# Expert stage with 160 slots per expert and a quarter-row tail, and a last stage written out tile by tile

## What is computed

```python
gp = softmax(hf @ w_group + b_group);  g_w, g_idx = top_k(gp, 1)
el = (hf @ w_router + b_router).reshape(T, 4, 8) taken at g_idx
e_val, e_idx = top_k(el, 2);  gate = softmax(e_val) * g_w      # 2 of 32 experts a token
y = (silu(xb @ w_gate[e]) * (xb @ w_up[e])) @ w_down[e]        # 1024 -> 512 -> 1024
h = h + sum of gate * y over the token's two experts
out = rms_norm(h, final_norm_w)
```

## Time and profile before

| | us |
|---|---|
| median of 3 runs | 1985.79 (1985.59 to 1987.25) |
| the profiled execution | 1985.4 |
| its span | 1983.6 |
| PE busy | 1793.7 (90%) |
| DVE / ACT / POOL busy | 619.7 / 501.0 / 231.4 |
| mixer, routing and first gather, experts, last stage | 0 to 1006, to 1060, to 1874, to 1983.6 |

### The profile page before, as it was taken

The page is one execution under the profiler, slowest core; times in us unless marked ns, Lnnn a source line. Parts: engine busy times, 40 slices in busy tenths (PEclk is TensorE's granted clock), DMA queues, the critical chain, the costliest instruction groups (busy, mean ns, idle before and its releaser), DMA issues.

```text
span 1983.6 us, 29788 instructions
## 1 busy us (share of the span) xinstructions
PE 1793.7 (90%) x10758; PEld 1285.1 (65%) x10759; DVE 619.7 (31%) x1155; ACT 501.0 (25%) x1173; POOL 231.4 (12%) x319
## 2 busy tenths in 40 slices
PE   7999999999999999999837999999999999999700
PEld 4656666656666656666426778887887888888500
DVE  1333323333224333324362222222221222222265
ACT  0433434233424333333300111111111111111121
POOL 0000101100101100101011000000000000000175
PEclk9999999999999999999858999999999999999955
DMA  9522112222012222022175788888887988888576
GB/s 324 135 85 86 36 50 84 85 85 85 23 62 85 85 85 75 21 73 85 64 271 168 261 302 294 281 303 306 300 304 263 318 303 299 301 296 291 185 255 222
DMA packets 194491, 358.65 MB, mean 181 GB/s; under 512 B 12179, under 2 KB 81444, under 8 KB 194452
## 3 DMA queue, kind: packets, MB, share of 16 engines
q1 hardware_dynamic: 183812, 320.93, 47.8%
q0 software_dynamic: 10640, 37.17, 6.2%
HBM read 280.73 MB, written 77.33 MB: 181 GB/s over the span
## 4 chain that ended last, share of the span: by engine, by line
PE 39%; issue 5%; DVE 2%; POOL 2%; DMA 1%; ACT 1%; POOLq 0%; ACTq 0%; SPq 0%; DVEq 0%
PE bank L1075 12%; PE bank L1100 11%; PE bank L1064 11%; PE bank L1049 3%; PE bank L1089 1%; POOL wts L1211 1%; DMA wts<-y_dram,dc 1%; POOL fs L1220 0%; DVE column L945 0%; ACT sg L1109 0%; DVE place L945 0%; DVE y L1135 0%; PE bank L350 0%; POOL dc L1207 0%; DMA y_dram<-y 0%
## 5 line engine op out<-in xcount | busy, mean ns | idle before, releaser
L282 PE MATMUL bank<-w_in_sb,uT 128*128 128x512 f32 (+1 forms) x1024 | 379.8, 524 | 4.8 <-DMA w_in_sb<-w_in_in 4.8
L282 PEld LDWEIGHTS bank<-w_in_sb,uT 128*128 128x128 f32 x1024 | 176.6, 192 | 173.3 <-issue 167.2
L1064 PEld LDWEIGHTS bank<-xT,wts 128*128 128x128 f32 x2048 | 250.1, 192 | 33.0 <-issue 26.6
L1064 PE MATMUL bank<-xT,wts 128*128 128x128 f32 (+2 forms) x2048 | 256.1, 285 | 11.9 <-issue 8.6
L1075 PE MATMUL bank<-xT,wts 128*128 128x128 f32 (+2 forms) x2048 | 247.9, 282 | 0.0
L1075 PEld LDWEIGHTS bank<-xT,wts 128*128 128x128 f32 x2048 | 245.0, 191 | 0.0
L1100 PE MATMUL bank<-wts,hT 128*128 128x512 f32 x512 | 233.5, 599 | 0.0
L430 PE MATMUL bank<-w_out_sb,mixT 128*128 128x512 f32 x512 | 224.0, 596 | 0.8 <-ACT mixT L507 0.8
L1128 DVE TENSOR_TENSOR hT<-bank,sg 128x256 f32<-128x256 f32 x128 | 54.3, 424 | 445.3 <-PE bank L1075 445.3
L430 PEld LDWEIGHTS bank<-w_out_sb,mixT 128*128 128x128 f32 x512 | 96.7, 191 | 116.7 <-issue 116.7
L1100 PEld LDWEIGHTS bank<-wts,hT 128*128 128x128 f32 x512 | 92.1, 190 | 99.7 <-issue 97.6
(11 more groups left out here) (206 smaller groups left out, 1722.1 us busy)
## 6 DMA issues: line engine op xcount, KB each, us to landing
wts<-w_gate_in SPq DMA_DIRECT2D x32, 2048.0 KB, 9.6
wts<-w_up_in SPq DMA_DIRECT2D x32, 2048.0 KB, 8.7
wts<-w_down_in SPq DMA_DIRECT2D x32, 2048.0 KB, 10.5
y_dram<-nought SPq DMA_DIRECT2D x64, 512.0 KB, 6.0
y_dram<-y SPq DMA_DIRECT2D x32, 512.0 KB, 10.4
x_sb<-x_in SPq DMA_DIRECT2D x17, 512.0 KB, 4.0
w_in_sb<-w_in_in SPq DMA_DIRECT2D x4, 2048.0 KB, 12.4
h_sb<-x_in SPq DMA_DIRECT2D x16, 512.0 KB, 6.0
```

Source lines behind the costliest of these rows:

```text
L282: m = pe.matmul(bk[name][:, col:col + hi - lo], uT[:, k, :], w_in[:, k, lo:hi], start=k == 0, stop=k == KD - 1)
L1064: m = pe.matmul(G[m_ % 2][:, 0:w], wg[:, k, m_ * P:(m_ + 1) * P], xT[:, k, 0:w], start=k == 0, stop=k == KD - 1)
```

## The change

1. An expert has MAIN = 160 main slots. Rows past 160 go to an overflow block (NOV 25 instead of 16; NCOL 114 instead of 96). `WIDTHS` has 128, 144, 160 only. The part of `y` between slot 160 and 256 and both halves of the overflow blocks are cleared: 6 DMAs of 512 KB a tile instead of 4.
2. The tail (slots 128 to 159) is gathered as 128 quarter rows of 1 KB, on 128 partitions: partition 32 q + r gets quarter q of row r. The index for it is 4 token + q, made in routing by one more matmul with a new constant `rep` and three more DVE instructions.
3. PE then transposes 8 pieces of the main part and 2 of the tail, in three steps of 4, 4 and 2. Step 0 stands between up and down, steps 1 and 2 between the halves of down. DVE evacuates with two instructions of 512 and two of 128 columns.
4. POOL and SP don't read the class: POOL always issues a gather of 128 rows and one of 128 quarter rows, SP always stores 512 KB and four times 32 KB. `y`'s second half is written by ACT alone (256 columns).
5. The last stage has no loop. POOL uses `dest` itself as index; the mean goes to ACT (`scale` in the square, epsilon by an Identity); DVE uses `gates` itself. POOL issues gathers three tiles ahead.

The core of the diff (names of helpers and waits left out where they only follow):

```diff
+MAIN = 160
+NOV = 25
-WIDTHS = (P, P + TAIL // 2, P + TAIL, CAP)
+WIDTHS = (P, P + TAIL // 2, MAIN)
...
-            for b in (2 * (n * i + m) + 1, 2 * NE + n * i + m):
+            for b in (2 * (n * i + m) + 1, 2 * NE + 2 * (n * i + m), 2 * NE + 2 * (n * i + m) + 1):
...
+        pe.wait_ge(sem("idx_tail_ready"), 1)
+        pe.matmul(bank[3][:, 0:NE], rep[:, 0:P], idx_f[:, :], start=True, stop=True).then_inc(sem("idx_spread"), 1)
...
-        dve.tensor_copy(idx, bank[2][:, 0:NCOL]).then_inc(sem("idx_ready"), 1)
+        dve.tensor_copy(idx[:, 0:NCOL:2], bank[2][:, 0:NCOL:2]).then_inc(sem("idx_ready"), 1)
+        dve.tensor_copy(idx_f[:, :], bank[2][:, 1:2 * NE:2]).then_inc(sem("idx_tail_ready"), 1)
+        dve.tensor_copy(idx[:, 2 * NE + 1:NCOL:2], bank[2][:, 2 * NE + 1:NCOL:2])
+        v_.wait_ge(sem("idx_spread"), 1)
+        dve.tensor_scalar(idx[:, 1:2 * NE:2], bank[3][:, 0:NE], 4.0, rep[:, P:P + 1], ALU.mult, ALU.add)\
+            .then_inc(sem("idx_ready"), 1)
...
+    def store(sp, e):
+        stored = sem("m_y_stored")
+        sp.dma_start(rows_of(e * CAP, P), y[:, 0, :]).then_inc(stored, 16)
+        for j in range(4):
+            sp.dma_start(rows_of(e * CAP + P, TAIL)[:, j * CAP:(j + 1) * CAP], yt[j * TAIL:(j + 1) * TAIL, :]).then_inc(stored, 16)
...
+    def gather(po):
+        po.indirect_dma_start(out=xg[:, 0, :], in_=scratch["v2"], out_offset=None,
+                              in_offset=bass.IndirectOffsetOnAxis(ap=idxc[:, 0:1], axis=0)).then_inc(sem("m_xg_loaded"), 16)
+        po.indirect_dma_start(out=xt, in_=scratch["v2"].rearrange("t (q c) -> (t q) c", q=4), out_offset=None,
+                              in_offset=bass.IndirectOffsetOnAxis(ap=idxc[:, 1:2], axis=0)).then_inc(sem("m_xt_loaded"), 16)
...
+    def pe_x(pe, n, steps):
+        for j in steps:
+            if j == 0:
+                wait(pe, sem("m_xg_loaded"), 16 * (n + 1))
+                after(pe, "m_", "xT_ready", 3 * n)
+            if j == 2:
+                wait(pe, sem("m_xt_loaded"), 16 * (n + 1))
+                after(pe, "m_", "xT_ready", 3 * n + 1)
+            for c in range(4 if j < 2 else 2):
+                src = xg[:, 0, (4 * j + c) * P:(4 * j + c + 1) * P] if j < 2 else xt[:, c * P:(c + 1) * P]
+                m = pe.transpose(XB[j % 2][:, c * P:(c + 1) * P], src, ident)
+            m.then_inc(sem("m_x_done"), 1)
...
-        next_x((0, 1))
+        next_x((0,))
...
-                next_x((2, 3))
+                next_x((1, 2))
...
+    def pool_tiles(po):
+        def fetch(t):
+            b = t % NYG
+            wait(po, sem("sum_s_ready"), t - NYG + 1)
+            for n in range(2):
+                po.indirect_dma_start(out=yg[:, b, n, :], in_=scratch["y"], out_offset=None,
+                                      in_offset=bass.IndirectOffsetOnAxis(ap=dest[:, n * NT + t:n * NT + t + 1], axis=0))\
+                    .then_inc(sem(f"yg_loaded{b}"), 16)
+        for t in range(NYG - 1):
+            fetch(t)
+        for t in range(NT):
+            if t + NYG - 1 < NT:
+                fetch(t + NYG - 1)
+            po.wait_ge(sem("fmean_ready"), t + 1)
+            nc.gpsimd.tensor_tensor(fs[:, t, 1:2], fs[:, t, 0:1], fk[:, 1:2], ALU.pow).then_inc(sem("froot_ready"), 1)
+    def act_tiles(act):
+        act.wait_ge(sem("fk_ready"), 2)
+        for t in range(NT):
+            wait(act, sem("sum_s_ready"), t + 1)
+            act.activation(fjunk[:, t % 2, :], hc[:, t, :], ACT.Square, scale=D ** -0.5, accum_out=fs[:, t, 0:1])\
+                .then_inc(sem("fss_ready"), 1)
+            act.wait_ge(sem("fss_ready"), t + 1)
+            act.activation(fs[:, t, 0:1], fs[:, t, 0:1], ACT.Identity, bias=fk[:, 0:1]).then_inc(sem("fmean_ready"), 1)
+    def dve_tiles(v_):
+        def add(t):
+            b, ht = t % NYG, hc[:, t, :]
+            v_.wait_ge(sem(f"yg_loaded{b}"), 32 * (t // NYG + 1))
+            nc.vector.scalar_tensor_tensor(ht, yg[:, b, 0, :], gates[:, t, 0:1], ht, ALU.mult, ALU.add).then_inc(sem("sum_steps"), 1)
+            v_.wait_ge(sem("sum_steps"), t + 1)
+            nc.vector.scalar_tensor_tensor(ht, yg[:, b, 1, :], gates[:, t, 1:2], ht, ALU.mult, ALU.add).then_inc(sem("sum_s_ready"), 1)
+        add(0)
+        for t in range(NT):
+            if t + 1 < NT:
+                add(t + 1)
+            v_.wait_ge(sem("froot_ready"), t + 1)
+            wait(v_, sem(f"out_stored{t % 2}"), 16 * (t // 2))
+            nc.vector.scalar_tensor_tensor(oc[:, t % 2, :], hc[:, t, :], fs[:, t, 1:2], fw[:, :], ALU.mult, ALU.mult)\
+                .then_inc(sem("sum_o_ready"), 1)
```

More of the change, by code:

```diff
@@ L1005, in load @@
         sp.dma_start(dst, src.rearrange("e (k p) n -> p (e k) n", p=P)).then_inc(sem(f"{pre}{name}_loaded"), 16)
[L1007 to L1033, removed]
+    def rows_of(row, n):
+        return scratch["y"][row:row + n, :] if isinstance(row, int) else scratch["y"][bass.ds(row, n), :]
@@ new lines, in gather, with gather_over @@
+    def gather(po):
[3 more added lines that the diff above has]
+                              in_offset=bass.IndirectOffsetOnAxis(ap=idxc[:, 1:2], axis=0)).then_inc(sem("m_xt_loaded"), 16)
+    def gather_over(po):
+        for part in range(2):
+            po.indirect_dma_start(out=xg[:, part, :], in_=scratch["v2"], out_offset=None,
+                                  in_offset=bass.IndirectOffsetOnAxis(ap=idxc[:, part:part + 1], axis=0))\
+                .then_inc(sem("o_xg_loaded"), 16)
@@ L1097, in pe_chunk @@
         for half in range(2):
-            after(pe, pre, ("yA_taken", "yD_taken")[half], 2 * n)
+            after(pe, pre, ("yA_taken", "yD_taken")[half], n if half and pre == "m_" else 2 * n)
             for k in range(KF):
@@ L1112, in act_chunk, with dve_x, dve_x_over @@
             after(act, pre, "d_done", 3 * n + 2 - part)
-            act.activation(y[:, part, 0:512], (YB, G)[part][0][:, :], ACT.Copy).then_inc(sem(pre + "yA_taken"), 1)
-    def dve_x(v_, pre, n, steps):
+            if part and pre == "m_":
+                act.activation(yt, G[0][:, 0:CAP], ACT.Copy).then_inc(sem("m_yA_taken"), 1)
+            else:
+                act.activation(y[:, part, 0:512], (YB, G)[part][0][:, :], ACT.Copy).then_inc(sem(pre + "yA_taken"), 1)
+    def dve_x(v_, n, steps):
+        for j in steps:
+            after(v_, "m_", "x_done", 3 * n + j + 1)
+            after(v_, "m_", "u_done", 4 * n)
+            if j < 2:
+                nc.vector.tensor_tensor(xT[:, 4 * j:4 * j + 4, 0:P], XB[j][:, :].rearrange("p (a b) -> p a b", a=4),
+                                        norm2[:, 4 * j:4 * j + 4].unsqueeze(2).to_broadcast([P, 4, P]), ALU.mult)\
+                    .then_inc(sem("m_xT_ready"), 1)
+            else:
+                for c in range(2):
+                    m = nc.vector.tensor_tensor(xT[:, c::2, P:MAIN], XB[0][:, c * P:(c + 1) * P].rearrange("p (q r) -> p q r", q=4),
+                                                norm2[:, c::2].unsqueeze(2).to_broadcast([P, 4, TAIL]), ALU.mult)
+                m.then_inc(sem("m_xT_ready"), 1)
+    def dve_x_over(v_, n, steps):
+        pre = "o_"
         for j in steps:
@@ L1131, in dve_y @@
     def dve_y(v_, pre, n, part):
-        if part:
+        if part or pre == "m_":
             wait(v_, sem(f"{pre}y_stored"), 80 * (n + 1))
@@ L1287, in program @@
         with ExitStack() as mem:
-            (credit, load, store, clear_xg, gather, copy_index, pe_x, pe_chunk, act_chunk, dve_x, dve_h, dve_y) = \
-                experts(nc, sem, bank, A, K, scratch, weights, mem)
+            (credit, load, store, store_over, gather, gather_over, copy_index, pe_x, pe_x_over, pe_chunk, act_chunk,
+             dve_x, dve_x_over, dve_h, dve_y) = experts(nc, sem, bank, A, K, scratch, weights, mem)
         block = ctx.enter_context(nc.Block())
@@ L1310, in _ @@
             mix_sp_loads(sp)
-            for q in range(2):
-                sp.sem_inc(sem(f"out_stored{q}"), 16)
             for pre in ("m_", "o_"):
```

171 lines of the change are left out of this document (63 added, 108 removed).

## The result

| | before | changed |
|---|---|---|
| time, median of 4 runs | 1986.5 us (1985.6 to 1988.4) | 1942.7 us (1941.1 to 1948.3) |
| ratio, with its 95% interval | | 0.978 [0.976, 0.980] |
| profiled execution: its time, its span | 1985.4, 1983.6 | 1948.3, 1946.3 |
| routing begins (logits), us from the start | 1005.8 | 1008.8 |
| routing and first rows, until the first gate matmul | 53.99 | 54.24 |

What follows compares the result with a forecast made beforehand. PE was taken to bound the experts, with DMA close second, and POOL the last stage. Experts -13.3, routing +0.6 and last stage -14.0 took 1985.4 to 1958.7, so 1959 us; range 1947 to 1975.

Steps and rivals of the forecast that it cites:

- the gain between the halves: Experts, PE: two transposes fewer between the halves of down, with nothing else awaited, save 0.22 us an expert.
- the new wait for `hT`: Ahead of down, PE waits about 0.25 us for DVE; gain 0.17 us (class 128), 0.23 (class 144), not 0.44.
- right to charge 0: Experts, DMA: 15 small packets an engine at 0.09 us, 1.35 us per class 128 expert, just fit; cost 0.
- Rival B: Experts: DMA becomes the limit; packets at 0.33 us give +55, near 2020; mild form 1966. Chances 0.08 mild, 0.04 past the turn.
- its ends: Routing and first rows: net +0.6 us, with ends -2 and +4.
- 333 GB/s when full, and a tile's 1.57 MB take 4.7 us: Last stage: 266 GB/s at share 0.80 was scaled to a full DMA rate, giving a floor per tile.
- the slowest of these is the DMA: Last stage: DMA, not POOL or DVE, sets the pace; 4.85 us a tile instead of 5.91 saves 13.8 us.
- POOL's 4.4 us: Last stage: two gathers and the power, stretched by DVE's scaling and additions, end near 4.4 us a tile.
- DVE's 3 x 1.32 = 4.0: Last stage: DVE's three instructions a tile need 4.0 us.
- POOL sets this: Last stage before the change: POOL, in work or its own issue gaps, sets the 5.91 us between output tiles.
- Rival A: Last stage: POOL and DVE exclude each other, 6.3 us a tile, +5 us instead of -13.8, total about 1978; chance 0.11.
- Rival C: Both hidden costs are smaller: experts -21 us, last stage at 4.4 us a tile (-20), total 1945; chance 0.07.

Runs made afterwards that it cites:

- oc4: The changed kernel with eight transposes ahead of down and two between its halves, plus four output buffers instead of two: 1929.7 us, ratio 0.973.
- dest_copy: The changed kernel with the copy of the two index columns, and the wait for it, on POOL again: 1950.1 us, ratio 0.983.
- mean_pool: The changed kernel with mean and epsilon computed on POOL again: 1951.5 us, ratio 0.984.
- experts_only: The changed kernel with the old last stage (loop, copies, mean on POOL, gathers two tiles ahead): 1970.9 us, ratio 0.992.
- last_only: The kernel before with only the new last stage; experts, classes, clears and routing as before: 1958.5 us, ratio 0.986.
- short_add_oc4: The changed kernel with four output buffers and DVE's second addition cut to 8 of 1024 columns: 1932.8 us, ratio 0.974.

## Why the prediction was right in one half and wrong in the other

**Experts: 13.6 us for 13.3, the mechanism right, so close in part by luck.** The count of ten transposes, the gain between the halves (0.22, measured 4.41 - 4.19 = 0.22) and the new wait for `hT` came as worked out. The semaphore takes 0.13 us, not 0.06 (no row stood behind the 0.06), so the gain ahead of down in class 128 is 0.11 instead of 0.17; class 144 fell from 26.5 to 26.06 us, the 0.45 forecast. Class 128 fell by 0.33 instead of 0.39, class 160 by about 0.5. That makes some 12.4 us. What brings it to 13.6 had no term: the first gate at the low clock, 2.5 us lost, and some 3.7 us gained in the periods of experts 0 to 6 and 16. There PE waits ahead of a gate for something that the profile doesn't name, four times and 8.6 us before, three times and 6.6 us after.

**DMA of the experts: right to charge 0.** The share was forecast at 22.8 / 22.96 = 0.99; it is 0.95 to 0.96. Even the 0.09 us for a small packet was too much. Rival B needed 0.2 us and a wait of PE for weights; the profile names none. (One of the three waits without a name ends at 1091.40, and the `w_gate` load that this gate needs was issued at 1073.54 and landed 8.2 us later.)

**Routing: within its ends.** POOL's rounds grew from 2.38 to 2.62 us and DVE's from 2.22 to 2.61; ten transposes take 2.68 us instead of 3.70. The sum was +0.25 (+0.4 to +0.6 in the later traces with these stages).

**Last stage: the step that failed** is "333 GB/s when full, and a tile's 1.57 MB take 4.7 us", and with it "the slowest of these is the DMA". I divided 266 GB/s by a share of 0.80, as if the share were a used part of a fixed rate. It isn't: in the changed kernel the share is 0.94 to 1.01 while the gathers run alone at 280 to 343 GB/s, and 1.02 at 405 (418 in `oc4`) with gathers and stores together.

```profile
1870.00:1874.50 4.50, 0.00 (x0) 0.00 (x0) 0.00 (x0) 0.00 (x0) 3.28 (x5) 0.50 0.94 280
1874.50:1878.00 3.50, 0.00 (x0) 0.00 (x0) 2.57 (x2) 0.64 (x1) 2.89 (x3) 0.50 1.01 343
```

The trace of the kernel before already had a stretch above that "full" rate, in routing, with loads running:

```profile
1010.00:1045.00 35.00, 12.29 (x54) 9.83 (x54) 29.24 (x52) 0.22 (x1) 8.27 (x4) 0.55 0.97 369
```

That tile 1 stands 3.3 us behind tile 0 was read rightly and came again (1874.66 and 1878.01), but it bounds gathers only, 1.05 MB in 3.3 us; the stores' 0.52 MB came beside them and not on top. Even the fastest tile, 3.77 us, is 0.4 us longer than its gathers need by that. The difference of 13 tiles at 4.85 and at 3.94 is 11.8 of the 12.9 us that the stage's forecast lacked. Half of it is the DMA's floor: without it the next in the list, POOL's 4.4 us, would have set the pace (13 x 0.45 = 5.9 us). The other 6.0 us are that POOL's 4.4 didn't hold either. The Trainium skill, SBUF — State Buffer, section "SBUF: two separate sides", gives the DMA ports about 436 GB/s; by that figure an estimate of the floor is 1.57 MB / 436 GB/s = 3.6 us. The 418 GB/s of `oc4` stay under it and are the most that these windows show; no run here shows that the ports are what limits.

**POOL's 4.4 us a tile was a real state, but of other kernels.** The working assumed that a gather starts with DVE's scaling. This holds where POOL is last (4.27 us in `dest_copy`, 4.5 in `mean_pool`), and not where DVE is. DVE's 3 x 1.32 = 4.0 was the right bound, and it was listed.

**What the working left out** is the round. "POOL sets this" was read from rows in which POOL is never free. But the same work on POOL, three tiles ahead, takes 4.51 us a tile instead of 5.83, so most of what looked like POOL's time was its place in the order. Depth was changed from two tiles to three and had no term, and it is worth 14 to 17 us.

**Rival A fell**, as argued from the 1.28 us in the earlier trace rows: none of DVE's instructions on 1024 columns in the new stage takes over 1.31 us, so POOL's gathers don't hold a port against DVE. By the quoted rule of the Trainium skill the loser is blocked for the whole instruction. POOL does stand still until DVE's ends; DVE for POOL's, never. Rival C was right on the last stage's direction (pace under 4.4) and wrong on the experts (-21); that its 1945 us lies near the measured time is luck, two misses that cancel. The start cost more than I thought: last 512 KB store to first gather went from 3.97 to 4.80 us, +0.83 instead of the +0.25 net that I had taken. The stores' part was sized about right (+1.35 in `experts_only` for 1.2); the copy and its wait gave 0.50 in `last_only` where 0.95 was taken.

**Open.** The cause of the mixer's varying end (6 us between the earliest and the latest) was not looked for. Nor is it settled what limits the gathers alone at the stage's start, what PE waits for ahead of those three gates, or why the clock of the first gate rises later.

## What to carry to other kernels

A busy share of a queue is not a used part of a rate: before it is turned into a floor, look for the highest rate that any window of the trace reaches, and for reads and writes apart. For a pipeline with buffers, write down the round that a buffer makes and divide it by the number of tiles in it; a change of depth always has a term. And where PE waits for an evacuation anyway, work that must be done some time is cheapest there: four transposes moved into such a wait gave 12 us for two edited lines, most of it in the class where the wait was longest. Where a change shortens what an engine does right after a long idle time, look at its granted clock behind it: here 1 us less of transposes came with a first gate 2.5 us longer.

## What the runs showed of the hardware beyond that

- POOL's gathers (0.94 us alone) that start during one of DVE's instructions end 0.8 to 0.94 us after that one's end: up to 2.03 us by phase alone. A gather that is already running when DVE's instruction starts takes 0.93 to 0.99 us, and DVE's isn't lengthened either. In these runs a tile has steady paces of 3.8 to 3.9 us with DVE last and of 4.0 to 4.5 with POOL last, and less work on DVE can lead from the faster to the slower (`short_add_oc4`).
- Deeper prefetch raised a gather's landing from 7.1 to 7.6 us and an output store's from 5.1 to 6.5, and still gained, because the landing is shared by four tiles.
- A 128x128 transpose costs 0.11 to 0.125 us between matmuls and almost nothing in PE's wait (0.06 us for four in class 128).
- The same 64 gate matmuls take 7.74 us or 10.28 us by the granted clock at their start (1.00, or 0.50 for the first 6 us).
